# Half A's last feed-forward part as seven block products of 256 columns in place of eight of 512, with half B's residual in DRAM meanwhile

## The reference

```python
def swiglu_ffn(h, w_gate, w_up, w_down):
    return (jax.nn.silu(h @ w_gate) * (h @ w_up)) @ w_down
...
        xp = xp + mp
        xs = xs + ms
        xp = xp + swiglu_ffn(rms_norm(xp, g_ffn[i]), w_gate[i], w_up[i], w_down[i])
        xs = xs + swiglu_ffn(rms_norm(xs, g_ffn[i]), w_gate[i], w_up[i], w_down[i])
```

## Time and profile before

| what | value |
|---|---|
| median of 3 runs | 2162.99 us |
| the profiled execution, its own time | 2162.42 us |
| span of the profile, first to last instruction | 2160.6 us |
| mean granted TensorE clock, share of full speed | 0.998 |
| PE busy, PEld busy | 2136.2 us (99%), 1934.6 us (90%) |
| DVE, ACT, POOL busy | 1423.6, 1165.5, 1340.6 us |
| HBM read, written | 186.49 MB, 7.19 MB |

### The profile page before, as it was taken

How to read it: one execution, slowest core, us unless ns; L and a number is a source line. 1 busy time by engine, 2 the same in 40 slices (tenths; PEclk the granted TensorE clock), 3 DMA queues, 4 the chain that set the end, 5 groups by cost and what they waited for, 6 DMA issues and landing times.

```text
span 2160.6 us, 35879 instructions
## 1 busy us (share of the span) xinstructions
PE 2136.2 (99%) x13360; PEld 1934.6 (90%) x13360; DVE 1423.6 (66%) x2345; ACT 1165.5 (54%) x2023; POOL 1340.6 (62%) x812
## 2 busy tenths in 40 slices
PE   9899999999999999999999999999999999999999
PEld 8798877888889789999999898888888889999998
DVE  5998788863434578888886455455555257665665
ACT  7556664533424666777763466565656334444443
POOL 3787889976446557675766644343433455868775
PEclk9999999999999999999999999999999999999999
DMA  5112323332333523222234342222222223233232
GB/s 158 49 50 59 88 83 98 98 98 88 98 98 99 140 75 98 76 83 83 76 98 133 97 98 85 88 82 84 79 87 80 85 85 114 89 118 112 80 103 81
DMA packets 314938, 198.43 MB, mean 92 GB/s; under 512 B 41398, under 2 KB 287758, under 8 KB 314510
## 3 DMA queue, kind: packets, MB, share of 16 engines
q1 hardware_dynamic: 312888, 195.03, 30.7%
q10 hardware_dynamic: 1878, 1.11, 0.2%
HBM read 186.49 MB, written 7.19 MB: 90 GB/s over the span
## 4 chain that ended last, share of the span: by engine, by line
PE 85%; DVE 9%; POOL 2%; issue 2%; ACT 1%; DMA 0%; SPq 0%; DVEq 0%; POOLq 0%; ACTq 0%
PE ps L613 37%; PE ps L1051 10%; PE ps L969 9%; PE ps L873 7%; DVE ps L2331 4%; PE ps L1080 4%; PE ps L1007 4%; PE ps L880 4%; PE ps L1088 2%; PE ps L1015 2%; PE ps L844 1%; PE ps L829 1%; PE ps L647 1%; DVE hBl L2228 1%; PE ps L805 1%
## 5 line engine op out<-in xcount | busy, mean ns | idle before, releaser
L3078 POOL TENSOR_TENSOR wlo<-raw,whi 128x1024 fp32r<-128x1024 f32 x218 | 542.1, 2488 | 541.9 <-PE ps L613 325.7
L613 PE MATMUL ps<-hAh,whi 128*128 128x512 f32 x1056 | 410.1, 392 | 2.3 <-ACT hAh L1489 0.9
L613 PE MATMUL ps<-hAl,whi 128*128 128x512 f32 x1056 | 408.0, 390 | 0.2
L1438 ACT ACTIVATE whi<-raw 128x1024 fp32r<-128x1024 f32 x218 | 230.4, 1057 | 312.0 <-PE ps L613 176.3
L613 PE MATMUL ps<-hAh,wlo 128*128 128x512 f32 x1056 | 267.8, 396 | 0.0
L3213 POOL TENSOR_TENSOR wlo<-raw,whi 128x512 fp32r<-128x512 f32 x124 | 174.4, 1417 | 113.4 <-ACT whi L1944 103.6
L613 PEld LDWEIGHTS ps<-hAh,whi 128*128 128x128 f32 x1056 | 198.0, 188 | 46.0 <-ACT hAh L1478 1.7
L613 PEld LDWEIGHTS ps<-hAl,whi 128*128 128x128 f32 x1056 | 198.3, 188 | 41.7 <-DVE hAl L2228 1.2
L613 PEld LDWEIGHTS ps<-hAh,wlo 128*128 128x128 f32 x1056 | 194.9, 188 | 42.4 <-issue 4.1
L3109 POOL TENSOR_TENSOR accp<-accp,prod 128x574 f32<-128x574 f32 (+1 forms) x136 | 192.3, 1414 | 29.6 <-ACT prod L1572 18.3
L2426 DVE TENSOR_TENSOR xB<-ps,xB 128x544 f32<-128x544 f32 x184 | 132.4, 720 | 99.0 <-PE ps L613 42.4
(11 more groups left out here) (429 smaller groups left out, 5465.8 us busy)
## 6 DMA issues: line engine op xcount, KB each, us to landing
raw<-in_w_gate_dram SPq DMA_DIRECT2D x58, 512.0 KB, 3.8
raw<-in_w_up_dram SPq DMA_DIRECT2D x58, 512.0 KB, 3.8
raw<-in_w_down_dram SPq DMA_DIRECT2D x54, 512.0 KB, 3.5
raw<-in_w_pw_dram SPq DMA_DIRECT2D x38, 512.0 KB, 3.8
raw<-in_w_down_dram SPq DMA_DIRECT2D x44, 256.0 KB, 3.2
raw<-in_w_gate_dram SPq DMA_DIRECT2D x40, 256.0 KB, 2.9
raw<-in_w_up_dram SPq DMA_DIRECT2D x40, 256.0 KB, 2.9
raw<-in_w_qkv_dram SPq DMA_DIRECT2D x32, 256.0 KB, 3.6
```

The costliest lines, as they stand in the source:

```text
L613: ins = nc.tensor.matmul(o, wt[n % 2][:, P * k:P * (k + 1)], src[h][:, k, c0:c0 + w], start=start, stop=stop)
L1438: nc.scalar.activation(whi[n % 2][:], raw[n % 2][:], ACT.Copy).then_inc(w_hi, 1)
L3078: nc.gpsimd.tensor_tensor(wlo[n % 2][:], raw[n % 2][:], f(whi[n % 2][:]), ALU.subtract).then_inc(w_lo, 1)
```

## The change

The layer 1 feed-forward part of half A is written as block products. The first round stays as it was (four plain tiles), and rounds 1 to 10 have 14 block products of 12 matmuls on 256 columns each in place of 96 matmuls of 512. The code of `ffn_v` is made common to both halves by a class `Seven`, which holds what differs. Half B keeps its order. For half A:

- The seven run in the order A11, A22, A12, S3, S2, S4, S1. Gate and up of all rounds use the same banks (`v_bank`): 0 for a and c, 1 for d, 2 for f, 3 for b and e, 7 for g.
- Three of the four weight sums of a gate or up overwrite raw weights (S3, S2, S4); S1 has room of its own in `sq`.
- Scratch for t1 and t2 lies in half B's residual, which is written to `x_spill["B"]` during `qkv("B")` and read back in two parts of 1.1 MB around the last block product. The other scratch lies in room that is idle then.
- DVE has its own order for this part, `ffn_va`.
- In the last round no down projection stands between the block products and half B's output projection `wo`.
- The sample's two scores now go to one bank (bank 7 is taken), with a wait of PE on its own first product (`s_first`).
- The norm of half A before this part is done first and its rounding later, as half B's is, with the sums t1 to t4 made beside it.

```diff
+        class Seven:
...
+                else:
+                    self.win = self.win0 = ["A11", "A22", "A12", "S3", "S2", "S4", "S1"]
+                    self.sums0 = ["S1", "S3", "S2", "S4"]
+                    self.blocks = 18 * (NG - 2) + 14
+                    self.norms = 5
+                    self.vf = uvf[:]
...
+            if S.h == "A":
+                return {"a": 0, "c": 0, "d": 1, "f": 2, "b": 3, "e": 3}[z]
+            return {"a": 0, "c": 0, "b": 1, "e": 1, "d": 2, "f": 3}[z] ^ (2 * (G % 2))
...
-                        o = ps[:, 4 + 3 * s, 0:nk]
+                        o = ps[:, 4, 256 * s:256 * s + nk]
                         qh, ql = qsh[r, b, :], qsl[r, b, :]
                         kh, kl = (z[r, b, :] for z in (skh, skl))
+                        if s:
+                            ins.then_inc(s_first, 1)
+                            pe.wait_ge(s_first, b + 1)
...
                 for G in range(1, NG):
-                    v_products("G", G)
-                    v_products("U", G)
-                    nxt[0] = v_bank(G, "d")
-                    v_down(G - 1)
-                v_down(NG - 1)
+                    v_products(S, "G", G)
+                    v_products(S, "U", G)
+                    nxt[0] = v_bank(S, G, "d") if S.h == "B" else 0
+                    if S.h == "B" or G < NG - 1:
+                        v_down(S, G - 1)
+                if S.h == "B":
+                    v_down(S, NG - 1)
+                    return
+                wo("B")
+                down(1, "A", NG - 2, lambda: norm_mean("ffn1B"), 0)
+                down(1, "A", NG - 1, None, 2)
...
+                for d in range(2):
+                    wo_tile(d)
+                freed(sp, ("V", "A", "U", NG - 1, "b"))
+                sp.dma_start(x["B"][:, 4:8, :], x_spill["B"][:, 4:8, :]).then_inc(S.x_back[1], 16)
+                full(sp, ("V", "A", "U", NG - 1, "e"))
+                sp.dma_start(x["B"][:, 0:4, :], x_spill["B"][:, 0:4, :]).then_inc(S.x_back[0], 16)
+                for d in range(2, KD):
+                    wo_tile(d)
...
+            def ffn_va(S):
...
+                    v_weight_sum(S, j + 1, "S1")
+                    read_scores(att, cur, 1)
+                    if G > 1:
+                        v_sum_up(S, "G", G, "e")
+                        v_last_sums(S, "G", G)
+                    v_weight_sum(S, j + 1, "S3")
+                    v_weight_sum(S, j + 1, "S2")
...
             qkv("B", "ffn1A")
-            ffn(1, "A")
+            ffn_v(SEVEN["A"])
             last_ffn()
```

1062 lines of the change are left out of this document (574 added, 488 removed).

## The result

| | before | after |
|---|---|---|
| median | 2162.97 us | 2175.45 us (2173.74 to 2175.73, 4 runs) |
| ratio to before | | 1.0057, 95% interval 1.004 to 1.0075 |
| the profiled execution, and its span | 2162.42, 2160.6 us | 2173.74, 2171.9 us |
| DVE, POOL, ACT busy | 1423.6, 1340.6, 1165.5 us | 1555.7, 1441.2, 1219.8 us |

What follows compares the result with a forecast made beforehand. PE, busy in 99% of the span and holding 85% of the chain of waits, was taken as the bound. Terms −20.0 + 3.5 + 3.6 + 1.0 + 0.6 + 0.3 = −11.0 us gave 2152.0 us, range 2144.5 to 2160.0.

Steps and rivals of the forecast that it cites:

- The matmuls: Gate and up in rounds 1 to 10: 168 matmuls at 0.119 us, 2.0 us a round less, minus 20.0 us.
- DVE's load: Check on half A's rounds: DVE busy about 33 of 36.6 us, 90%, so not the bound.
- The residual's write and read: `xB` around half A's part: read costed at nothing; write together with the norm 0.3 us (0 to 1).
- The sample's scores: PE waits twice for its own product, 0.3 us each: loss of 0.6 us (0.2 to 1.0).
- (b): Rounds 2 to 10, banks between gate and up: waits for e sum and silu, 3.6 us (0 to 9).
- (a): Start of the first block round: loss of 3.5 us (1.5 to 6), taken from half B's start.
- (c): Last round into `wo`: second tile waits on the bank of up's d, loss of 1.0 us (0.4 to 2).
- Slower: Rival, between gate and up: DVE behind, stalls of 2.9 us a round, 26 in nine rounds, 2174 us; chance 0.06.

Runs made afterwards that it cites:

- turn_e_first: Kernel after, half A's rounds: third unit's probabilities ahead of second unit's output, gate's e sum and last sums ahead of second scores on DVE; 2170.59 us, 1.0039.
- sums_small: Kernel after with half A's 80 DVE weight sums on 2 columns in place of 512, output wrong; 2153.84 us, ratio 0.9964.
- sums_one_input: Kernel after with half A's weight sums replaced by a one-input DVE reduction, POOL's work unchanged, output wrong; 2155.53 us, ratio 0.9971.
- lows_small: Kernel after with POOL's low parts of half A's blocks on 32 columns of 512; 2149.70 us, ratio 0.9943.
- halved_in_nine: Kernel after with half A's low parts as two POOL operations of 256 columns, in rounds 1 to 9 alone; 2165.09 us, ratio 1.0014.

## Why the prediction was wrong

**What held.** The matmuls: a pace of 0.12 us was read in after, and with POOL out of the way five of the eight rounds are 36.7 us, against 36.6 forecast. DVE's load: 32.9 us a round against "about 33", but by luck. With small low parts it is 219.92 / 8 = 27.5, so the work is less than the 30 in the forecast and the hold-ups are 5.4 in place of its 3. The residual's write and read: nothing, half A's part begins at the same 1312.5 us, and moving the reads changes nothing. The sample's scores: two breaks of 0.21 us, under the 0.6 forecast.

**The step that failed is (b), the term of 0.4 us a round, where 2.6 were lost.** Three things in it were wrong.

1. "DVE has 36.6 − 33 = 3.6 us a round to spare and gets ahead during the down products." The load was right and the conclusion was not. DVE's spare time lies where it waits for PE, and in half A's order the 9.5 us from the second split of probabilities to the third have no gap. The load of a round says nothing on one stretch of it.
2. The sums were priced by half B's medians, as a length. They hold waits: with small low parts DVE's busy time is less by (263.4 − 219.9)/8 = 5.4 us a round, of which one-input sums alone win (263.4 − 241.1)/8 = 2.8, where the prediction had "some 3" for everything. Almost half of the 5.4 come in the burst (0.43 + 0.91 + 1.10 = 2.4 us in the fourth round), where ACT's roundings, late behind the table load, let POOL's low parts fall on DVE's sums.
3. The chain was followed from the e sum only. PE waits there for 0.4 us a round and a restart. The larger wait, 1.2 us a round, is for the probabilities. Their rounding on ACT and their split on DVE stand behind the held operations, and the prediction gave no price to what of attention is queued there.

**(a), the start: 3.5 (1.5 to 6) and 7.3 measured.** The waits of half B's start that the prediction lists add up to 3.3. Half B's start was the wrong model. With small low parts round 1 takes 34.0 us in place of 39.0, with one-input sums 36.1, with the first wait of 0.9 unchanged in all: 5 of the 7.3 us are POOL's low parts and the sums they hold, in a round in which POOL is busy 28 of 39 us.

**(c), into `wo`: 1.0 (0.4 to 2) and 3.4 measured.** The mechanism was another. The prediction looked at the bank of the product d; what was late is the weights, whose buffer in `raw` POOL's low parts held: the last one made from a raw tile ends at 1709.63 and the issue is at 1709.65. With small low parts the weights are in time, and then the wait for product d appears, at 1.6 us:

```profile
PE ps L676 <- DVE s L2800: 1.6, 1, 1.6
```

**The rival.** "Slower" was given 2174 at a chance of 0.06, and 2175.5 came. That the number is so near is luck. Its place (between gate and up, DVE behind with the sums) is right. Its price, 2.9 us a round, is near the 2.6 measured, but it is made of 1.9 ahead of up's second product, where the trace has 0.4, and 1.0 ahead of the down products, where it has under 0.1. turn_e_first shows besides that the e sum's place costs nothing in that order. The sentence on the Trainium skill that stood beside it ("SBUF — State Buffer", section "Who interferes with whom") should have moved the chance. That section says that a VectorE operation with two inputs in SBUF contends with GpSimd's reads, that one with at most one input there does not, and that a copy from SBUF to SBUF can. All three are in these runs: two inputs, 0.67 to 1.78 us; one input by reduction, 0.68 to 0.72; a copy of two elements, 0.15 to 1.29. The prediction had dismissed it because the medians of half B were below its worst case. A stretch of one round can be near the worst case when the mean is not: in the burst above three of four operations were held.

**What stays open.** How the loss of the start splits between the sums and the late low parts is known only from these two runs. Nor was it tried apart what the first silu's place is worth once nothing on DVE is held.

## What to carry to other kernels

Before work is moved to an engine that has room by its busy share, lay out the stretch in which that work falls, and ask what waits behind it there. Count each VectorE operation with both inputs in SBUF as able to last one GpSimd operation longer; if the two engines feed one another, expect them to meet. Where they do, shorter GpSimd operations cut the wait, and an input in PSUM or a reduction with one input avoids it; a copy from SBUF to SBUF did not. And look at the engine that feeds both: here a table load on ScalarE decided whether they met.

## What the runs showed of the hardware

DVE's hold-up ends with the GpSimd operation that runs: at most 1.1 us more for low parts of 512 columns, at most 0.6 with halves (0.671 to 1.258 for S1's sum). It does not depend on how much DVE has to do: two elements a partition waited as long as 512. It goes the other way too: the four low parts of the burst above took 1.28, 1.73, 1.74 and 1.48 us, where one has 1.30 as a rule, and the three long ones began while a two-input operation of DVE ran.

A stretch of low clock of some 3 us followed PE's wait ahead of `wo` in after. The granted clock is 0.66 in the mean of these 5 us; matmul pairs are 0.45 us apart in it in place of 0.25, so it is the lower level of 1.2 GHz for most of them, and 1.6 us are lost:

```profile
1716.00:1721.00 5.00, 5.00 (x30) 5.00 (x29) 1.77 (x1) 2.10 (x3) 4.17 (x2) 0.66 1.00 363
```

The kernel before has one like it in the last feed-forward part (0.67 from 1785 to 1790 us), behind 16 matmuls that took 3.0 us too long in seven small waits. After has the same small waits, from 1793.9 to 1797.9, and a clock of 1.00 in them and behind them. So the two stretches cancel in the sum, and why this one is missing in after stays open. At `wo` it came in twelve of the sixteen kernels built on after, counting after itself, behind waits of 2.0 to 3.9 us, and not in sums_small, sums_one_input, lows_small and halved_in_nine, behind waits of 1.6 to 2.9. In the profiled executions those four take 454.8 to 455.0 us from `wo`'s first matmul to the end, and after takes 456.3. So the clock is some 1.4 us of what they gain, and it has no part in the windows of rounds 2 to 9. For halved_in_nine the profiled execution is also the fastest of its ten, 3.4 us under their median.
